# Reordering the opening, the compression products, the memory norm and the sums of squares in a one-core decoder kernel

## Chip, cores and metric

One core of one Trainium2 chip runs the kernel in a single launch. The metric is the device time of that execution in microseconds; the time before is the median of three runs.

## What is computed

x (256 tokens, 1024 features) goes through a first block and two more layers, all in float32. The first block is a mixer, memory attention and a gated convolutional FFN; behind it come a short convolution layer and an mLSTM layer, with 16 meta tokens ahead of the sequence. The parts that the change touches are these, cut from the reference:

```python
h = rms_norm(x, mix_norm_pre[l])
proj = h @ w_in[l]     # q, kc, vc, ks, vs, kw, vw, gates, pool, u, v
...
r = kv.reshape(B, S // 16, 16, G, dk)                    # compress(): of kc and vc
blocks = jnp.concatenate([r[:, :-1], r[:, 1:]], axis=2) + pos
h = jax.nn.gelu(jnp.einsum('bclgd,ldh->bcgh', blocks, w1) + b1)
return jnp.einsum('bcgh,hd->bcgd', h, w2) + b2
...
h = rms_norm(x, mem_norm_pre[l])                         # norm of x1
m = rms_norm(mem, mem_norm_kv[l])
x = x + rms_norm(memory_attention(h, m, w_mq[l], w_mk[l], w_mv[l], w_mo[l]), mem_norm_post[l])
h = rms_norm(x, ffn_norm_pre[l])                         # norm of x2
```

A further rms_norm of this kind stands ahead of the convolution layer (h0) and ahead of the mLSTM (h1).

## The kernel before

**Chunks.** The weights are packed as 288 chunks of 128 x 1024 floats, in the order of use (`_LAYOUT`, L40). Each chunk passes through one of four slots: SyncE loads it (`load`, L497), ScalarE copies it to `w_hi`, rounded (`hi`, L647), VectorE forms the rest `w_lo = raw - w_hi` (`lo`, L1855), and TensorE multiplies. ScalarE's copy of chunk n waits until the product of chunk n-4 is done; the load of chunk n waits for `w_lo` of chunk n-4. The calls `ahead(n)` on ScalarE and VectorE prepare chunk n+3, so the place of each call in the program of an engine sets the order there. Each engine's program is written out by hand and works strictly in order; engines meet through counting semaphores.

**Products.** Activations are split the same way (XH and XL, AH and AL, MH and ML). A chunk of eight 128-row tiles is three products per tile (`three`, L1296 to L1302): high by high, low by high, high by low. `chunk` (L1324) waits for both parts of the weights and runs all eight; `high_first` (L1338) needs `w_lo` only for its last third.

**Opening.** SyncE issues the gains, chunk 0, the halves of x, then chunks 1 to 3. ScalarE splits chunk 0, then the eight tiles of x scaled by the gain (L745); VectorE follows with their rests (L1965). TensorE runs kc with a wait per tile of x, then vc, vs and vw, ks, kw, query 0 (`qa`), the mean squares of the memory, the compression, queries 1 to 3, the gates and the scores.

**Compression.** kc and vc are gathered into `RF` (128 x 1024), rounded to `AH[:, 2048:3072]` (L768), the rest to `AL` (L2003). For each of 16 steps three products with a stationary tile of 64 columns (L1434 to L1436) run against two chunks at once, 256 columns. The result `ch` (64 rows used) is turned by two transposes (L1443, L1444), goes through gelu on ScalarE, and through `cmp_w2` (L1451, L1454).

**Memory.** ScalarE squares the memory (L771). The reciprocal root is spread over the partitions (L1203), copied to `rstd_m` (L792), and VectorE multiplies gain and rstd in eight instructions, three and five (L2043). ScalarE rounds all of it in one instruction during head 0 (L874), GpSimd takes the rest in one instruction (L597). In GpSimd's queue the store of the relative bias (L588) and its four loads (L592), each behind the product of a named chunk, stand ahead of that.

**Heads.** For each of eight heads TensorE runs one weight chunk, the pv products of the head before, qk of the head after, a second chunk, then turns the probabilities (`turn`, L1519 on, transposes at L1526 to L1531). VectorE adds the bias, takes maxima, and after ScalarE's exponentials (L852) scales (L2217). In heads 1 and 2 the chunks are `sgu_u` and `pool`; VectorE takes them out of PSUM (L2171, L2178) at the end of the head, in `fill_late`. Products alternate between two PSUM accumulators, and each waits for the one before the last to be taken out.

**Sums of squares.** A norm needs the mean square of each token. `stat_x` (L1207) runs 32 small f32 matmuls, recorded as 64, four strips of each of eight tiles of squares (`sum_strips`, L1193). It serves x, x1, x2 and h0. `stat_sum` (L1215) takes one tile that GpSimd has added up from seven (`sum_squares`, L542, six adds chained by a semaphore) and the last tile of squares by itself; it serves h1. ScalarE makes the squares in pairs (L688) behind the updated x, which VectorE adds up (L1904, L1949), between rests (L1885).

## Time and profile before

| | us |
|---|---|
| median of three runs | 925.24 (925.12 to 925.93) |
| the profiled execution | 926.31 |
| its span | 924.6 |
| TensorE (PE) busy | 911.6 (99%), 6977 matmul records |
| VectorE (DVE) busy | 657.1 (71%) |
| ScalarE (ACT) busy | 533.1 (58%) |
| GpSimd (POOL) busy | 129.5 (14%) |
| mean DMA | 171 GB/s |

The profile is of one execution. Busy times are of the engine's own instructions; matmuls are pipelined, so that the record of one (0.28 us for 256 columns) is longer than the step from one to the next. L12 is line 12 of the kernel. A row of the timeline gives start, length, engine, line, operation, output and inputs, shapes and count, and in brackets how long the engine sat idle before it and what ended that.

### The profile page before, as it was taken

The numbers are of one execution on the slowest core, as the hardware profiler recorded it, in microseconds if no ns is written. First come the engines' busy times: TensorE is split into PE (matmuls) and PEld (weight loads), VectorE is DVE, ScalarE is ACT, GpSimd is POOL, SyncE is SP. The second block draws the span as 40 slices with busy tenths as digits, with TensorE's granted clock in tenths as the row PEclk, the third lists the DMA queues.
The fourth block names the chain that finished last, engine by engine and source line by source line (L and its number), as shares of the span: only waits on it lengthen the run. The fifth ranks groups of instructions, "written<-read, shape, count | busy, mean of one in ns | idle before, by whom it ended". The sixth has DMA issues, their size and how long they took to land.

```text
span 924.6 us, 19102 instructions
## 1 busy us (share of the span) xinstructions
PE 911.6 (99%) x6977; PEld 856.3 (93%) x6977; DVE 657.1 (71%) x1116; ACT 533.1 (58%) x905; POOL 129.5 (14%) x122
## 2 busy tenths in 40 slices
PE   8999999999999999999999999999999999999997
PEld 7997899998999999889999999999999998888886
DVE  4898877555899997447877777766577566767743
ACT  6767677445776676446444444444454567666643
POOL 2210011000055666000111111101010000000000
PEclk9999999999999999999999999999999999999999
DMA  8752425535356665762655555565465544454561
GB/s 298 260 187 97 155 93 167 174 115 179 124 169 192 200 205 179 229 188 97 196 174 175 176 178 172 175 198 178 142 199 178 170 145 142 159 170 160 182 198 52
DMA packets 45075, 157.91 MB, mean 171 GB/s; under 512 B 6067, under 2 KB 7219, under 8 KB 44764
## 3 DMA queue, kind: packets, MB, share of 16 engines
q1 hardware_dynamic: 44524, 155.56, 51.3%
q0 software_dynamic: 496, 1.59, 0.6%
q8 instruction: 38, 0.62, 0.3%
q14 instruction: 17, 0.14, 0.1%
HBM read 156.06 MB, written 1.06 MB: 170 GB/s over the span
## 4 chain that ended last, share of the span: by engine, by line
PE 93%; DVE 3%; ACT 2%; issue 1%; DMA 1%; SPq 0%; DVEq 0%; ACTq 0%
PE acc L1300 13%; PE acc L1302 13%; PE acc L1301 13%; PE scores L1300 6%; PE scores L1301 5%; PE scores L1302 5%; PE acc L1253 4%; PE acc L1255 4%; PE acc L1254 4%; PE scores L1255 2%; PE scores L1253 2%; PE scores L1254 2%; PE outs L1253 2%; PE outs L1255 2%; PE outs L1254 2%; PE acc L1375 1%
## 5 line engine op out<-in xcount | busy, mean ns | idle before, releaser
L1859 DVE TENSOR_TENSOR w_lo<-raw,w_hi 128x1024 fp32r<-128x1024 f32 x288 | 356.1, 1243 | 98.1 <-ACT w_hi L652 97.6
L652 ACT ACTIVATE w_hi<-raw 128x1024 fp32r<-128x1024 f32 x288 | 302.2, 1056 | 150.4 <-PE acc L1302 64.8
L1300 PE MATMUL acc<-XH,w_hi 128*128 128x256 f32 (+1 forms) x624 | 178.2, 286 | 1.4 <-DVE SQ L2171 1.1
L1301 PE MATMUL acc<-XL,w_hi 128*128 128x256 f32 (+1 forms) x624 | 175.8, 282 | 0.0
L1302 PE MATMUL acc<-XH,w_lo 128*128 128x256 f32 (+1 forms) x624 | 175.8, 282 | 0.0
L1300 PEld LDWEIGHTS acc<-XH,w_hi 128*128 128x128 f32 x624 | 117.4, 188 | 3.9 <-issue 2.1
L1300 PE MATMUL scores<-XH,w_hi 128*128 128x272 f32 (+1 forms) x424 | 120.2, 283 | 0.0
L1301 PE MATMUL scores<-XL,w_hi 128*128 128x272 f32 (+1 forms) x424 | 119.7, 282 | 0.0
L1302 PE MATMUL scores<-XH,w_lo 128*128 128x272 f32 (+1 forms) x424 | 119.7, 282 | 0.0
L1301 PEld LDWEIGHTS acc<-XL,w_hi 128*128 128x128 f32 x624 | 117.5, 188 | 0.1
L1302 PEld LDWEIGHTS acc<-XH,w_lo 128*128 128x128 f32 x624 | 117.4, 188 | 0.0
L1300 PE MATMUL acc<-AH,w_hi 128*128 128x272 f32 (+1 forms) x360 | 103.9, 289 | 0.0
L1302 PE MATMUL acc<-AH,w_lo 128*128 128x272 f32 (+1 forms) x360 | 102.5, 285 | 0.0
L1301 PE MATMUL acc<-AL,w_hi 128*128 128x272 f32 (+1 forms) x360 | 102.5, 285 | 0.0
L1300 PEld LDWEIGHTS scores<-XH,w_hi 128*128 128x128 f32 x424 | 79.7, 188 | 0.2
L1301 PEld LDWEIGHTS scores<-XL,w_hi 128*128 128x128 f32 x424 | 79.8, 188 | 0.0
L1302 PEld LDWEIGHTS scores<-XH,w_lo 128*128 128x128 f32 x424 | 79.8, 188 | 0.0
L1300 PEld LDWEIGHTS acc<-AH,w_hi 128*128 128x128 f32 x360 | 68.0, 189 | 0.1
L1301 PEld LDWEIGHTS acc<-AL,w_hi 128*128 128x128 f32 x360 | 68.0, 189 | 0.0
L1302 PEld LDWEIGHTS acc<-AH,w_lo 128*128 128x128 f32 x360 | 68.0, 189 | 0.0
L629 POOL TENSOR_TENSOR AR<-AR,rstd 128x272 f32<-128x272 f32 x16 | 26.1, 1633 | 216.6 <-DVE AR L2363 216.6
L606 POOL TENSOR_TENSOR AR<-AR 128x256 f32<-128x256 f32 x22 | 32.3, 1470 | 131.6 <-DVE AR L2320 127.0
(533 smaller groups left out, 1797.1 us busy)
## 6 DMA issues: line engine op xcount, KB each, us to landing
raw<-weights SPq DMA_DIRECT2D x288, 512.0 KB, 3.6
cst<-params SPq DMA_DIRECT2D x1, 1080.5 KB, 8.8
XR<-x_t SPq DMA_DIRECT2D x2, 512.0 KB, 6.4
Y<-mem_t SPq DMA_DIRECT2D x1, 1024.0 KB, 7.6
AR<-bias_rows POOLq DMA_DIRECT2D x4, 256.0 KB, 6.4
out<-AR SPq DMA_DIRECT2D x2, 512.0 KB, 2.7
AR<-final_gain POOLq DMA_DIRECT2D x1, 512.0 KB, 7.5
cst<-params SPq DMA_DIRECT2D x1, 114.5 KB, 3.6
```

The source lines that it names most:

```text
L606: nc.gpsimd.tensor_tensor(Ft[:, p % 2, :], Gt[:, p % 2, :], Vt[:, p % 2, :], ALU.mult).then_inc(act_ready, 1)
L629: nc.gpsimd.tensor_tensor(Yc, Yc, rstd[:, :], ALU.mult).then_inc(c_scaled, 1)
L652: nc.scalar.activation(w_hi[:, n % SLOTS, :], raw[:, n % SLOTS, :], ACT.Copy).then_inc(hi_ready, 1)
L1253: nc.tensor.matmul(o, hi, w_hi[:, w, c], start=first, stop=False)
L1254: nc.tensor.matmul(o, hi, w_lo[:, w, c], start=False, stop=False)
L1255: return nc.tensor.matmul(o, lo, w_hi[:, w, c], start=False, stop=last)
L1300: nc.tensor.matmul(o, wh, h, start=start, stop=False)
L1301: nc.tensor.matmul(o, wh, l, start=False, stop=False)
L1302: return nc.tensor.matmul(o, wl, h, start=False, stop=stop)
L1375: nc.tensor.matmul(o, xh(k)[:, b * P:(b + 1) * P], wh, start=(k == 0), stop=False)
L1859: V.tensor_tensor(w_lo[:, s, :], raw[:, s, :], w_hi[:, s, :].bitcast(F32), ALU.subtract).then_inc(lo_ready, 1)
```

## The change

The diff does seven things.

1. SyncE issues the first half of x ahead of chunk 0. ScalarE and VectorE split chunk 0 between the fourth and fifth tile of x. A new `first_chunk` runs the products with `w_hi` of four tiles, then those with `w_lo`, then the other four tiles.
2. Query 1 moves ahead of the compression (`qa` has two chunks, `qb` two); chunk numbers shift, and the bias loads wait for other chunks. VectorE prepares chunk 8 after the keys instead of before.
3. High and low part of the compression input lie side by side in AH, 64 and 64 columns, so each step has one stationary tile of 128 columns and two products (with `w_hi` and `w_lo`). `ch` then has 128 rows; four f32 products with the identity add the halves and turn them.
4. The memory norm goes from VectorE to GpSimd: eight multiplies by the gain ahead of the bias loads, eight by rstd behind them, and the rest in eight pieces.
5. The spread of the memory's rstd moves between the two compression pairs; query 3 moves ahead of `cmp_w2`.
6. `keep_gated` takes the first tile of `sgu_u` and `pool` out before the head's exponentials are awaited, the second right behind the scaling.
7. The sums of squares of x1, x2 and h0 are added up by GpSimd and go through `stat_sum`.

```diff
-_LAYOUT = [("kc", 1), ("vc", 1), ("vsw", 2), ("ks", 1), ("kw", 1), ("qa", 1), ("cmp", 4), ("qb", 3), ...
+_LAYOUT = [("kc", 1), ("vc", 1), ("vsw", 2), ("ks", 1), ("kw", 1), ("qa", 2), ("cmp", 4), ("qb", 2), ...
...
+        RF_hl = AH[:, 2048:4096].rearrange("p (a b c) -> p a b c", a=16, b=2)
...
+            load_x(0)
             load(0)
-            load_x(0)
             load_x(1)
... (GpSimd)
             pool.dma_start(bias_rows, vec[0:HEADS, :]).then_inc(bias_stored, 16)
+            pool.wait_ge(mem_sq, 1)
+            for k in range(KT):
+                nc.gpsimd.tensor_tensor(mem_raw[:, k, :], mem_raw[:, k, :], col("g_mem_kv", k).to_broadcast([P, S]), ALU.mult).then_inc(mem_scaled, 1)
             pool.wait_ge(bias_stored, 16)
-            for j, done in enumerate((CHUNK["qa"], CHUNK["cmp"] + 1, CHUNK["cmp"] + 3, CHUNK["qb"])):
+            for j, done in enumerate((CHUNK["qa"], CHUNK["qa"] + 1, CHUNK["cmp"] + 1, CHUNK["cmp"] + 3)):
...
+            pool.wait_ge(mem_rstd, 1)
+            pool.wait_ge(mem_scaled, KT)
+            for k in range(KT):
+                nc.gpsimd.tensor_tensor(mem_raw[:, k, :], mem_raw[:, k, :], rstd_m[:, 0:S], ALU.mult).then_inc(mem_normed, 1)
             pool.wait_ge(mem_hi, 1)
-            nc.gpsimd.tensor_tensor(ML[:, :, :], mem_raw, MH[:, :, :].bitcast(F32), ALU.subtract).then_inc(mem_lo, 1)
-            pool.wait_ge(mem_lo, 1)
+            for k in range(KT):
+                nc.gpsimd.tensor_tensor(ML[:, k, :], mem_raw[:, k, :], MH[:, k, :].bitcast(F32), ALU.subtract).then_inc(mem_lo, 1)
+            pool.wait_ge(mem_lo, KT)
             nc.gpsimd.memset(pT[:, :, 0:META], 0.0).then_inc(pool_padded, 1)
             sum_squares(lambda m: wait_evacuated(pool, TILE["w_out"] + m), META)
+            for count in (1, 2):
+                sum_squares(lambda m: pool.wait_ge(sq_ready, KT * count + m + 1), META)
...
+            sum_squares(lambda m: pool.wait_ge(sq_ready, KT * 3 + m + 1), 0)
             with pool.Fori(0, E_TILES) as i:
... (ScalarE)
-            hi(0)
             act.wait_ge(gains_loaded, 16)
             for k in range(KT):
+                if k == KT // 2:
+                    hi(0)
...
-            ahead(CHUNK["cmp"] + 1)
+            ahead(CHUNK["cmp"])
             swap(0, "ks")
             swap(1, "kw")
+            ahead(CHUNK["cmp"] + 1)
+            act.wait_ge(rstd_spread, NORM_MEM + 1)
+            nc.scalar.activation(rstd_m[:, 0:S], spread_mem(), ACT.Copy).then_inc(mem_rstd, 1)
             for c in range(2, 4):
                 ahead(CHUNK["cmp"] + c)
-            ahead(query(1)[0])
-            act.wait_ge(rstd_spread, NORM_MEM + 1)
-            nc.scalar.activation(rstd_m[:, 0:S], spread_mem(), ACT.Copy).then_inc(mem_rstd, 1)
... (TensorE)
+            def first_chunk(n, t):
+                s, o, half = n % SLOTS, acc(t)[:, 0:S], KT // 2
+                pe.wait_ge(hi_ready, n + 1)
+                for k in range(half):
+                    x_ready(k)
+                    nc.tensor.matmul(o, w_hi[:, s, k * P:(k + 1) * P], xh(k), start=(k == 0), stop=False)
+                    nc.tensor.matmul(o, w_hi[:, s, k * P:(k + 1) * P], xl(k), start=False, stop=False)
+                pe.wait_ge(lo_ready, n + 1)
+                for k in range(half):
+                    nc.tensor.matmul(o, w_lo[:, s, k * P:(k + 1) * P], xh(k), start=False, stop=False)
+                for k in range(half, KT):
+                    x_ready(k)
+                    last = three(o, n, k, xh(k), xl(k), False, k == KT - 1)
+                last.then_inc(chunk_done, 1)
...
-            chunk(CHUNK["kc"], TILE["kc"], xh, xl, S, ready=x_ready)
+            first_chunk(CHUNK["kc"], TILE["kc"])
...
+            chunk(*query(1), xh, xl, S)
             pe.wait_ge(cmp_in, 1)
...
-                    rows = slice(2048 + 64 * j, 2048 + 64 * (j + 1))
-                    nc.tensor.matmul(o, AH[:, rows], slots(w_hi, n, cols), start=(j == 0), stop=False)
-                    nc.tensor.matmul(o, AL[:, rows], slots(w_hi, n, cols), start=False, stop=False)
-                    last = nc.tensor.matmul(o, AH[:, rows], slots(w_lo, n, cols), start=False, stop=(j == 15))
+                    both = RF_hl[:, j, :, :].rearrange("p a b -> p (a b)")
+                    nc.tensor.matmul(o, both, slots(w_hi, n, cols), start=(j == 0), stop=False)
+                    last = nc.tensor.matmul(o, both, slots(w_lo, n, cols), start=False, stop=(j == 15))
                 last.then_inc(chunk_done, 2)
-            pe.wait_ge(bias_copied, 1)
-            chunk(*query(1), xh, xl, S, between=lambda: spread_rstd(NORM_MEM, S, spread_mem()))
+                if c == 0:
+                    pe.wait_ge(bias_copied, 1)
+                    spread_rstd(NORM_MEM, S, spread_mem())
+            chunk(*query(2), xh, xl, S)
...
-            nc.tensor.transpose(OB[1][:, 0:32], ch[0:32, 0:P], ident[0:32, 0:32])
-            nc.tensor.transpose(OB[0][:, 0:32], ch[32:64, P:S], ident[32:64, 32:64]).then_inc(cmp_hidden, 1)
-            chunk(*query(2), xh, xl, S)
+            for bank, cols, at in ((OB[1], slice(0, P), 0), (OB[0], slice(P, S), 32)):
+                for part in range(2):
+                    last = nc.tensor.matmul(bank[:, 0:32], ch[:, cols], ident[:, 64 * part + at:64 * part + at + 32],
+                                            start=(part == 0), stop=(part == 1))
+            last.then_inc(cmp_hidden, 1)
+            chunk(*query(3), xh, xl, S)
...
-            stat_x(NORM_X1, 1, S)
+            stat_sum(NORM_X1, 2, lambda: pe.wait_ge(sq_ready, 2 * KT), S)
... (the same for NORM_X2 and NORM_H0)
... (VectorE)
-            lo(8)
... (behind keep_keys)
+            lo(8)
             lo(9)
             lo(10)
...
+            def keep_gated(h, j):
+                if h == 1:
+                    n, t = CHUNK["sgu_u"] + j, TILE["sgu_u"] + j
+                    wait_chunk(dve, n)
+                    freed(V.tensor_tensor(uT[:, j, :], acc(t)[:, 0:S], rstd[:, META:T], ALU.mult), t)
+                if h == 2:
+                    n, t = CHUNK["pool"] + j, TILE["pool"] + j
+                    wait_chunk(dve, n)
+                    if j == 0:
+                        dve.wait_ge(mem_lo, KT)
+                    freed(V.tensor_tensor(pT[:, j, META:T], acc(t)[:, 0:S], rstd[:, META:T], ALU.mult), t)
...
                 if h:
                     fill_dve(h - 1)
+                keep_gated(h, 0)
                 dve.wait_ge(exped, h + 1)
...
+                keep_gated(h, 1)
                 if h == 0:
                     compressed_probs()
```

## Rows read from the trace of the kernel before

**Rows 1.** The page: busy time by engine, and the two costliest groups of instructions.

```profile
PE 911.6 (99%) x6977; PEld 856.3 (93%) x6977; DVE 657.1 (71%) x1116; ACT 533.1 (58%) x905; POOL 129.5 (14%) x122
...
L1859 DVE TENSOR_TENSOR w_lo<-raw,w_hi 128x1024 fp32r<-128x1024 f32 x288 | 356.1, 1243 | 98.1 <-ACT w_hi L652 97.6
L652 ACT ACTIVATE w_hi<-raw 128x1024 fp32r<-128x1024 f32 x288 | 302.2, 1056 | 150.4 <-PE acc L1302 64.8
```

**Rows 2.** The waits of PE: for whom, us in total, times, longest.

```profile
PE acc L1300 <- DVE SQ L2171: 1.1, 1, 1.1
PE acc L1300 <- DVE Y L2178: 1.0, 1, 1.0
```

**Rows 3.** The timeline of the opening, ScalarE and PE.

```profile
7.69 3.31 ACT L745 ACTIVATE XH<-XR,cst 128x256 fp32r<-128x256 f32 x8 [1.52 <-DMA XR<-x_t]
...
12.08 0.31 PE L1343 MATMUL acc<-XH,w_hi 128*128 128x256 f32 x1
```

**Rows 4.** The instructions of line 504: ns min/median/max, first and last start.

```profile
L504 SPq DMA_DIRECT2D XR<-x_t x2: 426/466/507, 1.7 to 2.2; - x2
...
DMA to landing us min/median/max: 5.9/6.4/6.8
```

**Rows 5.** The timeline around the compression, PE and ScalarE.

```profile
34.17 0.30 PE L1434 MATMUL acc<-w_hi,AH 128*64 128x256 f32 x1 [0.20 <-DVE AR L2009]
...
39.83 0.28 PE L1436 MATMUL acc<-w_lo,AH 128*64 128x256 f32 x1
...
53.18 1.86 PE L1466 MATMUL turned<-AR 128*128 128x32 f32 x16
...
38.41 1.74 ACT L780 ACTIVATE SQ<-AR 64x256 f32<-64x256 f32 x4
```

**Rows 6.** The instructions of line 606, feed-forward stage: ns min/median/max.

```profile
L606 POOL TENSOR_TENSOR AR<-AR x22: 739/1586/1597, 253.2 to 361.6; 128x256 f32<-128x256 f32 x22
```

**Rows 7.** The timeline of GpSimd, and of VectorE in head 1.

```profile
44.09 0.71 POOL L592 DMA_DIRECT2D AR<-bias_rows  x1 [2.96 <-PE acc L1302]
65.15 4.59 POOL L597 TENSOR_TENSOR ML<-Y,MH 128x2048 fp32r<-128x2048 f32 x1 [20.35 <-ACT MH L874]
...
67.46 3.37 DVE L1859 TENSOR_TENSOR w_lo<-raw,w_hi 128x1024 fp32r<-128x1024 f32 x1 [0.23 <-ACT w_hi L652]
```

**Rows 8.** The page's DMA issues: KB each, median us to landing.

```profile
AR<-bias_rows POOLq DMA_DIRECT2D x4, 256.0 KB, 6.4
```

**Rows 9.** The timeline of head 2, VectorE and PE.

```profile
80.50 1.01 DVE L2217 TENSOR_SCALAR AR<-AR 128x128 f32<-128x128 f32 x4
...
81.62 0.38 PE L1526 MATMUL turned<-ident,AR 128*128 128x128 f32 x2
```

**Rows 10.** The timeline of PE at the sums of squares.

```profile
157.61 1.10 PE L1193 MATMUL outs<-SQ,ones_d 128*32 128x64 f32 x64
158.65 0.38 PE L1300 MATMUL acc<-XH,w_hi 128*128 128x256 f32 x1
...
243.52 1.10 PE L1193 MATMUL outs<-SQ,ones_d 128*32 128x64 f32 x64
...
430.37 1.15 PE L1193 MATMUL outs<-SQ,ones_d 128*32 128x68 f32 x64
...
663.75 0.33 PE L1193 MATMUL outs<-cst,ones_d 128*32 128x68 f32 x8
...
664.12 0.39 PE L1300 MATMUL acc<-XH,w_hi 128*128 128x272 f32 x1
```

**Rows 11.** The timeline of ScalarE at the last squares of x1, x2, h0.

```profile
156.04 0.91 ACT L687 ACTIVATE XH<-XR,cst 128x256 fp32r<-128x256 f32 x2 [0.15 <-DVE XR L1904]
156.86 0.61 ACT L688 ACTIVATE SQ<-XR 128x512 f32<-128x512 f32 x1
...
239.95 0.61 ACT L688 ACTIVATE SQ<-XR 128x512 f32<-128x512 f32 x1
...
426.33 0.64 ACT L688 ACTIVATE SQ<-XR 128x544 f32<-128x544 f32 x1
```

More of the change, by code:

```diff
@@ L1456, in _ @@
             last.then_inc(cmp_out, 1)
-            chunk(*query(3), xh, xl, S)
             chunk(CHUNK["gates"], TILE["gates"], xh, xl, S)
@@ L1684, in _ @@
             side_by_side(3, CHUNK["up"], TILE["up"], up_acc, xh, xl, RAW_X2)
-            stat_x(NORM_X2, 2, S)
+            stat_sum(NORM_X2, 3, lambda: pe.wait_ge(sq_ready, 3 * KT), S)
             ffn_pe(0, 3, lambda: spread_rstd(NORM_X2, S))
@@ L1696, in _ @@
             side_by_side(3, CHUNK["conv_in"], TILE["conv_in"], conv_acc, xha, xla, RAW_H0)
-            stat_x(NORM_H0, 3, T)
+            stat_sum(NORM_H0, 4, lambda: pe.wait_ge(sq_ready, 4 * KT), T)
             conv_pe(0, 3, lambda: spread_rstd(NORM_H0, T))
@@ L2032, in _ @@
             invert_root(NORM_MEM, S)
+            keep_query(1)
             n, t = CHUNK["cmp"], TILE["cmp"]
-            ahead(n + 1)
-            ahead(n + 2)
+            for c in range(3):
+                ahead(n + c)
             wait_chunk(dve, n + 3)
-            freed(V.tensor_copy(ch[0:64, :], acc(t)[0:64, 0:S]), t)
+            freed(V.tensor_copy(ch, acc(t)[:, 0:S]), t)
             ahead(n + 3)
-            def normalise_mem(first, end):
-                for k in range(first, end):
-                    last = V.scalar_tensor_tensor(out=mem_raw[:, k, :], in0=mem_raw[:, k, :], scalar=col("g_mem_kv", k),
-                                                  in1=rstd_m[:, 0:S], op0=ALU.mult, op1=ALU.mult)
-                    if k < KT - 1:
-                        chain.note(last)
-                return last
-            keep_query(1)
-            ahead(query(1)[0])
-            dve.wait_ge(mem_rstd, 1)
-            normalise_mem(0, 3)
             keep_query(2)
             ahead(query(2)[0])
+            keep_query(3)
             dve.wait_ge(cmp_out, 1)
@@ L2632, in _pack_weights @@
     queries = [_tiles(np, q, p) for p in pairs]
-    parts += queries[0:1] + pairs_of("cmp", hidden) + queries[1:4] + [narrow(gt, ar(24))] + pairs_of("sgu_v", lin(v)) + lin(u) + lin(pin)
+    parts += queries[0:2] + pairs_of("cmp", hidden) + queries[2:4] + [narrow(gt, ar(24))] + pairs_of("sgu_v", lin(v)) + lin(u) + lin(pin)
     mv = lin(a["w_mv"][0])
```

36 lines of the change are left out of this document (12 added, 24 removed).

## The prediction

> **What bounds the kernel now.** The profiled execution took 926.31 us, of which 924.6 us is its span; the median of the three runs is 925.24 us. I make the sum against 926.31 and move the result down by 1.07 us to stand with the median. I read the busy shares first: PE is busy 99% of the span [rows 1], so nothing but PE's own products, and the few places where PE waits, can move the end. Then the waits of PE: after the start only two exceed half a microsecond, 1.1 us on a VectorE copy into SQ and 1.0 us on one into Y [rows 2]. Last the timeline of each stage that the diff touches. A difference of 0.2% (1.85 us) is about what a measurement of this kernel can tell from no change.
>
> **Opening.** x now goes out ahead of the first weight tile. Before, ScalarE's copies of x began at 7.69 and took 3.31 us for eight, 0.41 each [rows 3]. The halves of x were issued at 1.7 and 2.2 and landed 5.9 and 6.8 us later, at 7.6 and 9.0 [rows 4]. The three transfers carry the same bytes after, so the last of them, x's second half, still lands near 9.0; only the first half moves, to some point ahead of 7.6. ScalarE's last four copies then end no sooner than 9.0 + 1.65 = 10.65, and VectorE, with w_lo of chunk 0 (1.24) [rows 1] now between its two halves, ends its rests near 11.3. The second chunk, which began at 12.08 [rows 3], begins near 11.75. **Gain 0.3** (0 to 1.0 if the second half lands early too). Cost of the moved weight load: load 4 waits for that w_lo and goes out about 2 us later, hidden behind the three tiles still queued.
>
> **Compression.** 48 products become 32. They run from 34.17 to 39.83, 47 steps, 0.12 us each [rows 5]; with low and high parts side by side in one stationary tile the form is 128 columns, as in all other chunks. Sixteen fewer: 1.93 us. The two small transposes, one pass each, become four f32 products of 128x32 of two passes each; 16 such passes took 1.86 us, 0.116 each [rows 5], so six more cost 0.70. The chunk ahead of it waited 0.20 us for VectorE's key copy [rows 5]; one w_lo moves behind that copy, and the wait goes. Net 1.93 - 0.70 + 0.20 = 1.43.
> What is late next: weight preparation. Chunk 11's slot is free only when the query ahead of the pairs is done. PE then needs it after 16 products and the spread, 1.92 + 1.0 = 2.9 us; ScalarE's copy (1.06) and VectorE's rest (1.24) take 2.3 [rows 1], but the vector queue still holds a query copy and a reciprocal, and GpSimd now runs eight multiplies here. For the next query ScalarE passes four half-tile swaps (1.74 us) [rows 5] before its copy: about 3.2 us against 2.9. I take stalls of **0.8** in all (0 to 1.4). **Gain 0.6** (0 to 1.4).
>
> **Memory normalised by GpSimd.** VectorE loses eight multiplies; GpSimd gets sixteen, and its one subtraction of 4.59 us becomes eight. 4.59 / 8 = 0.57 us per tile; an operation on 256 columns with the port to itself is recorded as 0.74 [rows 6]. The first pass, 5 to 9 us from about 34, stands ahead of the four bias loads in GpSimd's queue; they end near 46.5 instead of 44.8 and land some 6.4 us later [rows 7, 8], before the softmax of head 0 asks near 55. The second pass ends by 55; ScalarE reads the result near 62. So the cover is 7 us, and I cost the lateness at nothing. The contention is another matter: while the single subtraction ran (65.15 to 69.74) a w_lo that started at 67.46 took 3.37 us instead of 1.24 [rows 7, 1]: it stood still until GpSimd was through. Short GpSimd instructions hold it for 0.57 at most, which takes back the small wait ahead of turn(1): **gain 0.25** (0 to 0.3). The last bias load took GpSimd 0.71 us [rows 7], and I cost all four so.
> The Trainium skill (SBUF — State Buffer, section "SBUF: two separate sides") says a load issued by GpSimd grows from about 620 to 3100 ns beside a VectorE copy. By that the four would take 12.4 us and head 0 would wait several us for its bias; the row with 0.71, beside a w_lo on VectorE, decides here.
>
> **Gated tiles sooner.** The 1.1 us and 1.0 us waits [rows 2] are accumulators whose product was long done, freed only at the end of a head. Both go. But after the first, PE reaches turn(2) (81.62) with its probabilities just made, 80.50 to 81.51 [rows 9], by a ScalarE chain (two table loads, four exponentials) that hangs on turn(1), not on this wait. Of 1.1 about **0.45** remains; of the second **1.1** (its next turn has over a microsecond of room). Sum 1.55 (1.0 to 2.2).
>
> **Squares added by GpSimd.** A stage of `stat_x` occupies PE from 157.61 to 158.65, 1.04 us; the two-part form, already used near the end, from 663.75 to 664.12, 0.37 us [rows 10]. Three stages save 0.67 each, if the sum is there. Before x2 and h0 the last squares end at 240.56 and 426.97, PE asks at 243.52 and 430.37 [rows 11, 10]: 3 us of room for at most three adds at 0.74. Gain **1.35** together (-2.5 to 1.35).
> Before x1 there is no room: the last squares end at 157.47, PE asks at 157.61 [rows 11, 10]. Without any contention the last add ends at 158.2, PE goes on at 158.6, and nothing is gained or lost. But there VectorE runs back to back, additions and rests with both inputs in SBUF, and ScalarE's copies for the last pair wait for it (0.15 us) [rows 11]. By the row at 67.46 each add holds VectorE up for 0.57. With turns taken one for one, three adds fall ahead of its last addition: squares near 159.4; the last two adds with one w_lo between them end near 161.0, PE goes on at 161.4. **Loss 2.6** (0 to 3.8).
>
> **Sum.** 0.3 + 0.6 + 0.25 + 1.55 + 1.35 - 2.6 = 1.45. 926.31 - 1.45 = 924.86, or 923.8 beside the median. Own range of this case: 922.3 to 925.3, 0.50, of which 0.10 lies over 0.2% faster.
>
> **Rivals.**
> (1) The port at x1 costs little: the adds slip into VectorE's PSUM reads. For: its scaling instructions read PSUM and, as elsewhere in the trace, were not held. Against: the 3.37 us row. Then x1 costs 0 to 0.5, compression perhaps 1.0: gain 4.3, 921.0. Chance 0.30, all faster.
> (2) Slower: the six chained adds at all three stages. In the feed-forward stage, beside a w_lo, GpSimd's instructions were recorded at 1.59 us in the median rather than 0.74 [rows 6]. At 1.6 per add the chain from the first pair takes 9.6 us: x1 loses 4, x2 (first squares 235.7) asks at 243.52 and gets its sum at 245.3, loses 1.1 net, h0 loses 0.8. That is -5.9 in place of -1.25; with compression at nothing the total is 3.8 slower, 929.0. It decides from an add of about 1.3 us on. Against: VectorE has pauses at x2 and h0 after its last w_lo. Chance 0.10.
> (3) The softmax chain takes all: the freed tiles bring nothing, since ScalarE's chain from turn to turn is the real bound of heads 1 to 3. Gain falls by 1.55 to -0.1: 925.3. Against: PE still has room at turn(3). Chance 0.10, all within 0.2%.
> The Trainium skill (SBUF — State Buffer, section "Who interferes with whom") says whoever issues first keeps the shared pair for its whole instruction; the 3.37 us row agrees. It says nothing of who is next among waiting ones, which is what parts the forecast from rival 1.
>
> **How the numbers follow.** Likeliest case 923.8. Faster: 0.30 + 0.10 = 0.40. Within 0.2%: 0.40 + 0.10, and 0.01 of rival 2's near end: 0.51. Slower 0.09. The range, 920.7 to 926.0, takes in rivals 1 and 3 and leaves out rival 2 and the outer tenth.
>
> **What would show it.** In the profile after: the second chunk begins at 11.5 to 12.0; 32 compression products, with waits of PE on w_lo of 0.3 to 1.4 us around them; no wait on SQ or Y copies in the heads, but one of about 0.5 at turn(2) on VectorE; no w_lo over 2.5 us near 65; a wait of PE on GpSimd's sum before mq of 2 to 3 us (under 0.9: rival 1), none before the feed-forward and convolution (over 1 us: rival 2). I am wrong if waits of PE on w_lo appear beyond 100 us, or if the opening moves by over 1 us.

## The result, and the profile after

| | before | after |
|---|---|---|
| median, us | 925.57 (925.12 to 926.12) | 938.86 (931.3 to 939.6, five runs) |
| ratio | | 1.0127 [1.0105, 1.0149] |
| the profiled execution, us | 926.31 | 931.3 |
| its span, us | 924.6 | 929.4 |

The change makes the kernel slower: by 1.3% in the ratio, by 13.3 us between the medians, where 1.45 us of gain was forecast. The profiled execution of the changed kernel is its fastest; the other four lie at 938.4 to 939.6. So the same kernel was run and profiled again (experiment e0, 936.38 us in that execution), and the two profiles are read side by side. What both show is taken as the price in every execution. What e0 alone shows is taken as what makes most of them slower still, and the mean granted clock of the runs speaks for that: 0.992 to 0.994 of 2.4 GHz in the four slower ones, 0.993 in e0's, 0.997 in that of 931.3.

The page of the execution of 931.3 us. GpSimd has 160.4 us for 129.5 [rows 1], PE 154 fewer records, and yet PE is busy for longer.

```profile
PE 914.3 (98%) x6823; PEld 858.6 (92%) x6823; DVE 661.4 (71%) x1108; ACT 532.8 (57%) x905; POOL 160.4 (17%) x163
L1893 DVE TENSOR_TENSOR w_lo<-raw,w_hi 128x1024 fp32r<-128x1024 f32 x288 | 356.8, 1246 | 95.1 <-ACT w_hi L665 94.6
```

The waits of PE after its start, same execution (for whom; us in total, times, longest). Both waits of [rows 2] are gone, the one of 0.5 at a turn is there (0.6), and a new one of 3.0 on GpSimd's sum for x1.

```profile
PE outs L1207 <- POOL cst L549: 3.0, 1, 3.0
PE acc L1465 <- DVE AR L2063: 0.9, 1, 0.9
PE turned L1560 <- DVE AR L2241: 0.6, 1, 0.6
```

And those of e0, the same kernel at 936.38 us. The first row is new: PE stands 4.7 us ahead of the first compression product, until VectorE has freed query 1's accumulator.

```profile
PE acc L1465 <- DVE AR L2063: 4.7, 1, 4.7
...
PE outs L1207 <- POOL cst L549: 3.0, 1, 3.0
PE acc L1314 <- DVE AR L2063: 0.9, 1, 0.9
```

Where PE stands at six places, read from the timelines, in us. Differences between neighbouring columns say in which stretch the time went.

```text
                              before   after    e0      e17 (best version, below)
sum of x                       17.38    17.34   17.54    17.37
first scores product, head 0   55.33    55.07   62.70    54.58
sums of y                     144.62   143.19  152.24   142.37
sum of x1                     157.61   159.25  168.28   155.37
sum of x2                     243.52   245.58  254.91   241.39
last product                  919.09   923.90  929.07   916.70
```

Three losses can be read off it. (1) In e0, 7.4 us up to head 0, and 1.5 more by the scores of head 1 (62.03 before, 70.94). (2) At x1 about 3 us, in both. (3) From x2's sum to the end: 675.6 us before, 678.3 in the execution of 931.3, but 674.2 in e0. The last is not a wait: the timeline has none there.

**Loss 1, at the memory norm.** GpSimd's and VectorE's timelines in the execution of 931.3: start, length, engine, line. GpSimd's eight gain multiplies take 7.67 us, 0.96 each, and VectorE's three w_lo 4.42. They take turns: a multiply beside a w_lo is recorded at about 1.6 us, one alone at about 0.6, and no w_lo there takes over 1.73.

```profile
33.95 7.67 POOL L593 TENSOR_TENSOR Y<-Y,cst 128x256 f32<-128x256 f32 x8
32.81 4.42 DVE L1893 TENSOR_TENSOR w_lo<-raw,w_hi 128x1024 fp32r<-128x1024 f32 x3
44.55 7.37 POOL L604 TENSOR_TENSOR Y<-Y,rstd_m 128x256 f32<-128x256 f32 x8
```

The same in e0. Now the eight run in 4.60 us, 0.57 each, with nothing between them, and VectorE's two w_lo of 34.44 take 6.86 instead of 2.4: the first of them takes 5.72 and stands still for the whole series. The same happens at 50 us, in the second series.

```profile
34.47 4.60 POOL L593 TENSOR_TENSOR Y<-Y,cst 128x256 f32<-128x256 f32 x8
34.44 6.86 DVE L1893 TENSOR_TENSOR w_lo<-raw,w_hi 128x1024 fp32r<-128x1024 f32 x2 [0.25 <-ACT w_hi L665]
50.02 5.58 POOL L604 TENSOR_TENSOR Y<-Y,rstd_m 128x256 f32<-128x256 f32 x8
50.17 6.52 DVE L1893 TENSOR_TENSOR w_lo<-raw,w_hi 128x1024 fp32r<-128x1024 f32 x1 [0.21 <-ACT w_hi L665]
```

**What a pause costs besides itself.** PE in e0, and by stretch (us; busy of PE, PEld, DVE, ACT, POOL; then PEclk, the granted clock as a share of 2.4 GHz; DMA). Behind the pause the clock is 0.50, 1.2 GHz: products 0.21 us apart instead of 0.12, until about 46.7, some 5 us of work that cost 2.5 more.

```profile
41.77 0.55 PE L1465 MATMUL acc<-w_hi,AH 128*128 128x256 f32 x1 [4.71 <-DVE AR L2063]
...
44.26 0.41 PE L1466 MATMUL acc<-w_lo,AH 128*128 128x256 f32 x1
44.47 0.41 PE L1465 MATMUL acc<-w_hi,AH 128*128 128x256 f32 x1
...
42.00:46.00 4.00, 4.00 (x20) 4.00 (x21) 1.50 (x3) 0.38 (x1) 0.17 (x1) 0.50 0.96 305
46.00:48.00 2.00, 2.00 (x16) 2.00 (x16) 1.22 (x1) 1.64 (x3) 0.55 (x1) 0.82 0.98 371
```

**Loss 2, at x1,** execution of 931.3: PE asked at 156.3 and waited 2.99 us for GpSimd's last add, and here too the clock fell behind the pause. The strip took 0.59 us instead of 0.37, and the next eleven steps 2.44 instead of 1.30: 1.4 more.

```profile
152.79 1.23 DVE L1938 TENSOR_TENSOR XR<-XR,Y 128x512 f32<-128x512 f32 x1
155.63 3.56 POOL L549 TENSOR_TENSOR cst<-cst,SQ 128x256 f32<-128x256 f32 x3 [2.16 <-ACT SQ L701]
156.01 1.75 DVE L1893 TENSOR_TENSOR w_lo<-raw,w_hi 128x1024 fp32r<-128x1024 f32 x1
159.25 0.44 PE L1207 MATMUL outs<-cst,ones_d 128*32 128x64 f32 x8 [2.99 <-POOL cst L549]
...
160.00:162.00 2.00, 2.00 (x10) 2.00 (x11) 1.32 (x3) 1.72 (x3) 0.00 (x0) 0.50 0.40 141
```

**Loss 3, the spacing of products.** The same stretch of the feed-forward loop, before and after, PE 100% busy at a clock of 1.00 in both: 796 products against 767 in 90 us.

```profile
260.00:350.00 90.00, 90.00 (x796) 90.00 (x795) 84.34 (x136) 63.12 (x103) 54.42 (x34) 1.00 0.61 198
```

```profile
260.00:350.00 90.00, 90.00 (x767) 90.00 (x766) 80.30 (x131) 60.52 (x98) 50.13 (x33) 1.00 0.56 187
```

The starts of successive products lie 0.1133 us apart before and 0.1178 after, all through the loop (means over 946 and 950 steps, from 250 us on). 960 products by 0.0045 us is 4.3 us; less the 1.35 that the two shorter sums save, this makes 2.9, beside the 2.75 by which the stretch from x2's sum to the end is longer in the execution of 931.3. e0 has the shorter spacing: it lost more in front and less here. Both levels occur in either kernel in earlier stages; what differs is which one the loop is run at.

### The profile page after: what moved, and what is told of

It reads as the page before. It is cut to its first block, busy times and chain, and to the rows that moved or that the text cites. A ratio compares the mean times of both kernels' runs of the same rounds, so it can differ in the third digit from the quotient of the medians.

```text
span 929.4 us, 18833 instructions
## 1 busy us (share of the span) xinstructions
PE 914.3 (98%) x6823; PEld 858.6 (92%) x6823; DVE 661.4 (71%) x1108; ACT 532.8 (57%) x905; POOL 160.4 (17%) x163
## 3 DMA queue, kind: packets, MB, share of 16 engines
q0 software_dynamic: 496, 1.59, 0.6%
## 4 chain that ended last, share of the span: by engine, by line
PE 91%; DVE 4%; ACT 2%; issue 1%; DMA 1%; POOL 0%; SPq 0%; DVEq 0%; ACTq 0%; POOLq 0%
PE acc L1314 13%; PE acc L1316 13%; PE acc L1315 13%; PE scores L1314 6%; PE scores L1316 6%; PE scores L1315 6%; PE acc L1269 4%; PE acc L1267 4%; PE acc L1268 4%; PE scores L1269 2%; PE scores L1268 2%; PE scores L1267 2%; PE outs L1269 2%; PE outs L1268 2%; PE outs L1267 2%; DVE w_lo L1893 1%
## 5 line engine op out<-in xcount | busy, mean ns | idle before, releaser
L642 POOL TENSOR_TENSOR AR<-AR,rstd 128x272 f32<-128x272 f32 x16 | 26.2, 1634 | 156.3 <-DVE AR L2388 156.3
L1269 PE MATMUL acc<-w_hi,AL 128*128 128x512 f32 x128 | 49.9, 390 | 0.0
```

Source lines behind the costliest of these rows:

```text
L642: nc.gpsimd.tensor_tensor(Yc, Yc, rstd[:, :], ALU.mult).then_inc(c_scaled, 1)
L1269: return nc.tensor.matmul(o, lo, w_hi[:, w, c], start=False, stop=last)
```

## The experiments

The first theory, on record ahead of e0 to e3, was built on the execution of 931.3 alone: x1's sum comes late, the pause brings the clock down, and perhaps the loop's spacing hangs on it. It had nothing at the memory norm. The theory that the later runs test has three sources. A, a back-to-back series of GpSimd holds VectorE's w_lo up, as if the whole series were one instruction; B, x1's chained adds come too late; and both pauses bring the clock down; C, the spacing of the loop's products turns. In the expectations "theory A" is the theory of that run, and what it says stands beside it. Rivals are named with each run. Diffs are against the changed kernel unless said otherwise.

**e0, the changed kernel again; e1, x1's sum back on TensorE; e2, all three sums back; e3, the kernel before with one more warming product.**

```diff
# e1 (e2 does the same at x2 and h0)
-            stat_sum(NORM_X1, 2, lambda: pe.wait_ge(sq_ready, 2 * KT), S)
+            stat_x(NORM_X1, 1, S)
# e3, against the kernel before, ahead of the feed-forward loop
-            keep_warm(1, PTB)
+            keep_warm(2, PTB)
```

> The changed kernel as it is, for the spread of its times and a second trace. Theory A (three costs in a row: PE waits 3.0 us for GpSimd's sum before mq; this pause drops the granted clock to half for 3.4 us; the feed-forward loop then runs at 0.1178 us per 256-column product instead of 0.1133, 4.3 us): the trace shows the wait of 3 us again, and the times that lie near 939 are those in which the clock stays at half for longer than 3.4 us. Rival B (something far from the norm, for example weight preparation late in the long loops): waits of PE on w_lo beyond 250 us that the first trace does not have.

> The changed kernel with the sum of squares before mq on PE again (stat_x), the other two still with GpSimd. Theory A: the 3 us wait goes, the clock stays at full speed, and about 2.65 + 1.7 us come back; if the pitch of the loop hangs on the pause too, another 4.3 us: 921 to 927, and all executions close together. Rival B: still above 930, or executions still 8 us apart.

> The changed kernel with all three sums of squares on PE again. Against e1 it should be 1.3 us slower if the sums before the feed-forward stage and before the convolution save 0.67 us each as worked out, and no different if they don't. If the pitch of the feed-forward loop flips with it, 4.3 us more or less on top, to be read from the trace.

> The kernel before with one more warming product (128 columns, two passes) ahead of the feed-forward loop, nothing else. If the pitch of the loop's products has two levels and what stands ahead of the loop picks one (theory C), its 960 products may run at 0.1178 us instead of 0.1133: 4.3 us slower, 929.5. If the level hangs on something else (the pause, the clock), this kernel costs only its own 0.15 us: 925.5.

Measured, beside 926.29 for the kernel before: e0 937.15 (ratio 1.0119 [1.0091, 1.0147]), e1 935.49 (1.0101 [1.0084, 1.0118]), e2 930.34 (924.83 to 933.08, 1.0039 [1.0019, 1.006]), e3 930.62 (1.0045 [1.0028, 1.0062]). e3 settles what the spacing is worth, and that one more small product ahead of the loop can turn it: its four runs lie at 930.19 to 932.18, the lowest three about 4 us above the kernel before, and its loop shows the spacing of after.

```profile
260.00:350.00 90.00, 90.00 (x767) 90.00 (x766) 79.63 (x131) 60.05 (x97) 49.54 (x33) 1.00 0.57 187
```

e0 has the wait of 3 us at x1 again and its low clock, as expected, but not the longer spacing, and no wait on w_lo beyond 250 us (rival B falls). What that theory had nothing about is the wait of 4.7.

e1 and e2 removed the wait at x1, and both traces brought the large wait at the compression (4.4 and 4.7 us), which the first profile hadn't shown. e1 missed its 921 to 927 by 8 us: its rival (still above 930) holds, and the x1 sum is not the main loss. e2 was expected 1.3 us above e1 and lies 5.1 below it. Its trace has the loop at 0.1133, that of e1 at 0.1178, so putting the sums of x2 and h0 back turned the spacing as well.

```profile
260.00:350.00 90.00, 90.00 (x797) 90.00 (x795) 84.67 (x138) 64.02 (x105) 53.74 (x35) 1.00 0.58 189
```

Two of e2's ten runs, at 924.83 and 925.01, had a mean clock of 0.999 and 1.000 where the other eight had 0.994 to 0.996. They have no profile, but it looks as if the series at the memory norm cost nothing in them.

**e6, GpSimd's gain multiplies spaced; e14, both series spaced; e15, both spaced and x1's sum on TensorE.**

```diff
# e6; e14 and e15 do the same in the second series, with mem_normed
             for k in range(KT):
+                if k:
+                    pool.wait_ge(mem_scaled, k)
                 nc.gpsimd.tensor_tensor(mem_raw[:, k, :], ... ALU.mult).then_inc(mem_scaled, 1)
```

> The changed kernel with one wait more: each of GpSimd's eight gain multiplies waits for the one before it, so the series is no longer queued back to back. Theory A (while a back-to-back series of GpSimd runs, VectorE's w_lo beside it stands still: it took 4.6 us in the executions near 937 and not in the one at 931.3): each gap lets VectorE in, no w_lo there takes over 2 us, TensorE's wait for the accumulator of query 1 (before the first compression product) is 0 to 1.2 us instead of 4.5, the clock holds at 2.4 GHz from 40 to 48 us, and the time is 930 to 933, in every execution. Theory B (who gets the port first is chance, spacing does nothing): the wait stays at 4.4 us and the time at 937 to 939.

> The changed kernel with both of GpSimd's memory series spaced: every multiply waits for the one before it. Theory A (back-to-back series lock VectorE out): no w_lo of over 2.5 us between 32 and 56 us, no wait of TensorE over 1.2 us before 60, the first scores product at 55 to 56.6, and a median of 930 to 933, no run over 936 but by a turned product spacing. Rival (spacing changes only the odds of one execution): 937 to 939 in half of the runs, and a w_lo of over 5 us in the trace.

> As e14, with the sum of x1's squares back on TensorE. It differs from e10_best (926.7, lowest 922.1) only in that GpSimd normalises the memory, spaced. Theory A (spaced, GpSimd's share costs what VectorE's turns beside it cost, 0.4 to 1.7 us a piece): 925 to 929. Rival (GpSimd's memory work costs the 4 us and the clock behind it whether spaced or not): 931 to 935, as e1 with the series unspaced (935.5).

Measured: e6 932.3 (928.41 to 939.61; 1.0049 [1.0034, 1.0063]), e14 932.14 (929.81 to 933.77; 1.0068 [1.0056, 1.008]), e15 928.77 (924.21 to 931.3; 1.0017 [1.0001, 1.0034]). A wait of each multiply for the one before, which adds work, makes the kernel 6.7 us faster: 938.86 to 932.14, and 935.49 (e1) to 928.77 (e15). The intervals of the ratios don't touch; against e0's median of 937.15 the first difference is 5.0. e14 and e15 lie in the ranges that theory A gave; e6's runs leave its 930 to 933 on both sides. e14's waits of PE and its w_lo beside the series:

```profile
PE outs L1211 <- POOL cst L549: 3.0, 1, 3.0
PE acc L1469 <- DVE AR L2067: 1.2, 1, 1.2
...
34.23 3.32 DVE L1897 TENSOR_TENSOR w_lo<-raw,w_hi 128x1024 fp32r<-128x1024 f32 x2 [0.25 <-ACT w_hi L669]
```

No w_lo stands still (the two take 1.77 and 1.63), and the 4.7 is 1.2. The same can be counted over all traces: beside eleven series of multiplies queued back to back (two each in after, e0, e1, e2 and e8, one in e6) seven times a w_lo took 3.4 to 6.8 us; beside five spaced ones (e6, e14, e15) the longest took 1.8. e6, which spaces the first series alone, has both in one trace. This is its second:

```profile
46.17 6.55 POOL L606 TENSOR_TENSOR Y<-Y,rstd_m 128x256 f32<-128x256 f32 x8
48.73 3.40 DVE L1895 TENSOR_TENSOR w_lo<-raw,w_hi 128x1024 fp32r<-128x1024 f32 x1 [2.37 <-ACT w_hi L667]
```

Being queued back to back is not enough by itself, though. The eight subtractions near 65 us, of the same shape and with no wait between them either, run beside a w_lo in fourteen traces, and it took 1.57 to 1.59 us in every one. This is that of the execution of 931.3:

```profile
64.89 6.60 POOL L607 TENSOR_TENSOR ML<-Y,MH 128x256 fp32r<-128x256 f32 x8 [12.96 <-ACT MH L888]
67.21 1.59 DVE L1893 TENSOR_TENSOR w_lo<-raw,w_hi 128x1024 fp32r<-128x1024 f32 x1 [0.23 <-ACT w_hi L665]
```

Behind e6's long w_lo PE waited 1.1 us at 54.3, and the clock fell. e6's one run at 939.61 was its profiled one. It has no long wait at the first compression product, but besides this one another kind of loss: from 455 to 677 us its products of 272 columns stood 0.1267 us apart, where every other trace has 0.1233 (1423 products against 1462 in 180 us). That is 1750 steps by 0.0033, 5.8 us.

```profile
460.00:640.00 180.00, 180.00 (x1423) 180.00 (x1422) 131.32 (x203) 74.79 (x92) 24.36 (x15) 1.00 0.53 175
```

**e8, the kernel before with only the memory norm moved to GpSimd; e7, the changed kernel with it back on VectorE; e9, e7 with x1's sum on TensorE too.**

```diff
# e7, e9: VectorE again, as in the kernel before
+            dve.wait_ge(mem_rstd, 1)
+            normalise_mem(0, 3)
             keep_query(2)
...
             ahead(query(3)[0])
+            normalise_mem(3, KT).then_inc(mem_normed, 1)
```

> The kernel before with the memory normalised by GpSimd as the change does it (gain multiplies ahead of the bias loads, reciprocal-root multiplies behind them), and nothing else. The prediction costed this at 0.25 and a gain of 0. Theory A (the series holds the port): a w_lo between 33 and 46 us takes 4 to 8 us, TensorE waits 3 to 4.5 us for w_lo or for an accumulator with a drop of the clock behind it, and the time is 928 to 933. Rival (the old order gives VectorE the slack that the new one takes): no wait over 1 us there, 925 to 926.

> The changed kernel with the memory normalised by VectorE, at the two places of the kernel before (three steps behind the compression's copy, five behind the compressed keys and values); everything else of the change stays. Theory A (GpSimd's memory work is what costs): the wait ahead of the first compression product is gone or under 1 us, the only long wait of TensorE left is the 3.0 us for the x1 sum with its 3.4 us at half clock, and the time is 929 to 932. Theory B (the reordered compression itself leaves VectorE late, GpSimd or not): the wait of over 3 us stays, and the time is 935 or more.

> The changed kernel with two parts undone: the memory normalised by VectorE, and the sum of x1's squares left to TensorE. What stays: opening, compression in two products, gated tiles, sums of x2 and h0 by GpSimd. If the two parts undone are the whole loss, the rest gives what was forecast for it: 0.3 + 0.6 + 1.55 + 1.35 = 3.8 at most, so 922 to 923.5 where the 256-column products of the feed-forward loop go 0.1133 us apart, and 926.5 to 928 where they go 0.1178 apart. If something else of the change also costs, 929 or more at the faster spacing.

e8: 926.43 (925.5 to 929.46; 1.001 [1.0001, 1.0019]). The mechanism shows in its purest form, with VectorE's instruction started 0.14 us before GpSimd's series and outlasting it:

```profile
44.50 5.57 POOL L602 TENSOR_TENSOR Y<-Y,rstd_m 128x256 f32<-128x256 f32 x8
44.36 6.79 DVE L1867 TENSOR_TENSOR w_lo<-raw,w_hi 128x1024 fp32r<-128x1024 f32 x1
...
PE acc L1308 <- DVE AR L2036: 1.4, 1, 1.4
```

but the old order of the compression leaves PE more work to do meanwhile. 0.6 us is lost between the medians, 0.9 by the ratio: the median lies below theory A's 928 to 933 and above the rival's 925 to 926, and the profiled run, at 928.05, has its wait of 1.4 with the clock at 1.00. e7 gave 933.64 (1.0072 [1.0057, 1.0087]) and e9 928.87 (1.0031 [1.0021, 1.0042]), 1.6 and 0.9 us above the upper ends of what was expected. The wait of 4.7 is gone, but the place that I gave the last five multiplies made the gates' evacuation late:

```profile
PE outs L1498 <- ACT AR L815: 1.5, 1, 1.5
...
48.00:60.00 12.00, 10.47 (x84) 9.53 (x83) 10.61 (x25) 5.71 (x10) 0.00 (x0) 0.86 0.57 203
```

A fault of my experiment, and a useful one: behind the short products here a pause of 1.5 us brings the clock to 0.50, for 3.4 us in e9's trace (0.86 over these 12) and for 6.8 in e7's. The place is fragile: in e3, whose code here is that of the kernel before, a pause of 0.47 was followed by the same in the profiled execution (932.18, the slowest of its four), so were e15's 0.6 and e6's 1.1, and e14's 0.6 was not. It is also where e0 lost its 1.5 us ahead of head 1.

**e4, x1's sum alone; e5, gated tiles alone; e12, compression alone; e13, opening alone** (each against the kernel before; e12 is the compression part of the diff with VectorE's five late multiplies right behind `keep_query(2)`, where it had been idle for 1.8 us; GpSimd's rest of the memory stays in eight pieces, as in the change).

> The kernel before with one edit: the squares of x1 added by GpSimd, TensorE's 64 one-column products replaced by one strip behind GpSimd's last add. The prediction's term: TensorE goes on 2.6 us late, 0.7 of it given back by the shorter sum. Theory A (the last three adds are held by VectorE's wide instructions, and the pause of 3 us brings TensorE's clock to 1.2 GHz for 3.4 us behind it, 1.7 us more): wait on GpSimd's add 2.5 to 3.1 us, clock row 160:164 under 0.8, time 928.5 to 930. Rival (the clock loss seen in the changed kernel comes from elsewhere in it): clock stays 1.00, time 927 to 928.

> The kernel before with one edit: the four gated tiles evacuated one at a time ahead of the softmax work. The prediction's term: waits of 1.1 and 1.0 at 73.8 and 83.5 gone, a new one of about 0.5 at the turn of head 2, together 1.55 gained: 923.9 to 924.3. In the changed kernel the landmarks moved by 1.34 and 0.34 at these two places, 1.7 in sum. Rival (ScalarE's softmax takes the gain, as the prediction's third rival has it): 925.3 or more. If the one-column or 256-column spacing flips behind it, 4.3 more on either.

> The kernel before with the compression part alone: two products of 128 rows a step, query 1 drawn ahead of it, hidden values as accumulated products; the memory normalised by VectorE at its idle times, opening, gated tiles and all sums as before. The prediction's term: 1.43 saved of products less 0.8 of stalls on w_lo, so 0.6 gained, 0 to 1.4: TensorE reaches the first scores product 0.6 earlier, 54.7 for 55.33, and the time is 925.1. Theory A (the traces of e10_best, where it came at 54.5 with the opening in it): 54.5 to 54.9. Rival (the w_lo stalls take all): 55.3 or later. If the 256-column level turns, 4.3 us more in the time, so that the landmark decides.

> The kernel before with the opening part alone: x ahead of the first weights on SyncE's queue, the first chunk's w_lo products of the first half behind its w_hi products. The prediction's term: 0.3 gained. In the changed kernel TensorE reached the sum of x at 17.34 for 17.38, so theory A says nothing is gained: landmark within 0.15 of 17.38, time within 0.2% of before. Rival (the prediction's): 17.1, time 925.3 to 925.5.

| | median, us | ratio | in the stretch behind it, by trace | forecast |
|---|---|---|---|---|
| e4 x1's sum | 930.94 (929.51 to 931.91) | 1.006 [1.0045, 1.0074] | 3.7 lost (sums of y to sum of x2: 98.9 before, 102.6) | 2.6 lost |
| e5 gated tiles | 924.90 | 0.9992 [0.9983, 1.0001] | 0.9 gained (144.62 to 143.70) | 1.55 gained |
| e12 compression | 924.81 | 0.999 [0.9981, 0.9998] | 1.05 gained (55.33 to 54.28) | 0.6 gained |
| e13 opening | 925.83 | 1.0001 [0.9993, 1.001] | nothing (17.38 to 17.39) | 0.3 gained |

Each of these stretches is read from one trace, and the same code doesn't come to the same place to within 0.3 us: e4, unchanged up to there, reaches head 0 at 54.87, e3 at 55.51, the kernel before at 55.33. The medians say the same as the traces for e5 (0.9 gained), e12 (1.1) and e13 (0.05).

e4 has the wait and the clock of loss 2 in a kernel that is otherwise the old one, so both belong to x1's sum (theory A there; the clock's rival falls):

```profile
PE outs L1194 <- POOL cst L547: 3.0, 1, 3.0
...
160.00:164.00 4.00, 3.58 (x32) 3.41 (x32) 3.32 (x4) 1.75 (x3) 0.36 (x1) 0.57 0.61 218
```

Its profiled run is the fastest of the four, 3.2 us above before's; the median is 5.2 above the one of its own round and 0.9 above the expected range, and what makes up the rest has no trace. In e5 both old waits go, and two new ones come at the turns of heads 1 and 2, since the evacuation now stands ahead of the scaling that PE waits for:

```profile
PE turned L1526 <- DVE AR L2219: 1.1, 2, 0.6
```

**e10, the best set; e11, the same with two warming products; e16, e10 without the opening; e17, compression and gated tiles alone** (with the norm on VectorE and the eight pieces as in e12).

```diff
# e10: e9, with the five late multiplies moved
             keep_query(2)
+            normalise_mem(3, KT).then_inc(mem_normed, 1)
             ahead(query(2)[0])
... (and gone from behind ahead(query(3)[0]))
```

> The last kernel (changed, memory normalised by VectorE, x1's sum on TensorE) with the five late memory steps moved from ahead of the gates' evacuation to VectorE's idle 1.8 us behind the evacuation of query 2. Theory A (those five steps made TensorE wait 1.5 us for the gates, and the clock at 0.86 from 48 to 60 us took 1.4 to 1.7 more): wait gone, clock 1.00, 3 us less: 925 to 926 where the feed-forward loop goes at 0.1178 us a product, 921 to 923 where it goes at 0.1133. Rival (the clock falls there for the accumulated small products, wait or not): clock stays at 0.86, 1.5 less: 926.5 to 928.5.

> The kernel of e10_best with two warming products ahead of the feed-forward loop instead of one. In the kernel before this alone turned the spacing of the loop's 256-column products from 0.1133 to 0.1178 us. Theory C (the level at the loop's entry is turned by what stands ahead of it): it turns here too, so that this kernel and e10_best lie 4.3 us apart, one at 921 to 923, the other at 925 to 927. Rival (in the changed kernel the level varies from execution to execution and the extra product does not decide it): both kernels show both groups of times, with medians within 1.5 us.

> The kernel of e10_best with the opening as before: compression in two products, gated tiles, sums of x2 and h0 by GpSimd, memory on VectorE, x1's sum on TensorE. The sum of what the traces gave for the parts: 1.05 + 0.92 + 1.32 = 3.3, so 922.5 where the feed-forward loop goes at 0.1133. Theory D (the opening sets the level's chance): all runs at 922 to 923. Rival (it is the sums or the gated tiles): runs between 922 and 929 as in e10_best, median 924 to 927.

> The kernel before with compression in two products and the gated tiles one at a time, and nothing else. 1.05 + 0.92 = 2.0 from the two parts alone, less if the second evacuation wait moves: 923.6 to 924.2 at 0.1133. Rival (two parts moved together already turn the level): 928 in some or all runs.

| | median, us | ratio | runs |
|---|---|---|---|
| e10 | 926.73 | 1.0008 [0.9997, 1.0019] | 922.06, 924.79, ten from 926.17 to 928.89 |
| e11 | 924.12 | 0.999 [0.9975, 1.0005] | six from 922.35 to 923.53, six from 924.71 to 928.58 |
| e16 | 926.57 | 0.9998 [0.9988, 1.0008] | 922.59, 922.93, ten from 926.17 to 927.24 |
| e17 | 923.89 | 0.9973 [0.9963, 0.9983] | nine from 923.22 to 923.99 |

In e10 the wait of 1.5 us is gone and with it the low clock, as its theory A had it, and the median is 2.1 us below e9's; at 926.73 it is 0.7 above the range for the longer spacing:

```profile
48.00:60.00 12.00, 12.00 (x110) 11.44 (x109) 11.18 (x31) 7.22 (x16) 0.00 (x0) 1.00 0.53 189
260.00:350.00 90.00, 90.00 (x766) 90.00 (x765) 80.03 (x131) 61.06 (x99) 49.23 (x34) 1.00 0.55 191
```

e10 and e16 have two groups of runs about 4 us apart, and e11's spread over the same stretch; the profile of e10 is one of 927.06 with the loop at 0.1178, that of e11 one of 922.72 at 0.1133. The warming product, decisive in e3, does not decide here: both groups occur with one and with two, as e11's rival has it, though with medians 2.6 us apart rather than 1.5. Whether it shifts the odds (one or two of e10's twelve runs in the fast group, six or seven of e11's) twelve runs don't show. e15 has the two groups too, three runs at 924.2 to 924.5 and nine from 927.03 up. The opening doesn't set them (theory D falls: two of twelve without it too). e17 lacks the sums of x2 and h0, and all its runs lie within 0.8 us, its trace at the shorter spacing. All traces taken together: with x2's sum added up by GpSimd the loop runs at 0.1178 in nine of eleven (not in e0 and e11), without it at 0.1133 in eight of nine (not in e3). So it is with the change of that sum, and of the products just ahead of the loop, that the second level comes in. Why is not shown. In the traces of e1, e9, e15 and e16 the loop's first 95 steps are of 0.1136, and the spacing turns to 0.1178 at one longer step of 0.21 to 0.22, where its second pass begins; in that of e10 it is 0.1178 from the start; in e0 the step there is 0.20 and nothing turns. **e17 beats both kernels**, 0.27% under the kernel before, inside the 923.6 to 924.2 that was expected from its two parts.

## Why the prediction was wrong

- **Memory normalised by GpSimd: the step that failed most.** It read a single instruction of 4.59 us rightly as one that holds a w_lo for its length, and concluded "Short GpSimd instructions hold it for 0.57 at most". Eight short ones, queued with nothing between, held a w_lo for 4.5 to 5.6 us, as if they were one. Spacing them gives back 6.7 us (5.0 against e0's median), and again 6.7 with x1's sum on TensorE; in e0's trace it is 4.7 of wait and 2.5 of clock. For the rest in eight pieces, near 65 us, the sentence held: the w_lo there takes 1.59 for the 3.37 of before. So the step that failed is that the bound of one short instruction was taken to hold for any series of them. The gain of 0.25 did not come: the small wait ahead of turn(1) is 0.20 after and 0.16 before. The passage on lateness ("I cost the lateness at nothing") looked at who waits for GpSimd, and not at who is held by it.
- **A pause has a second price.** No term had the clock in it. In the kernel before the granted clock was 1.00 up to the last 3 us, and after its start it had no pause of over 1.1 us; those of 4.7, 3.0 and 1.5 us in the later kernels were each followed by products at 1.2 GHz.
- **x1's sum.** "PE goes on at 161.4", a wait near 3 us: measured 3.0, with a w_lo beside the last adds, as in the working. PE came to this place 1.4 us sooner than before, and went on to its next product at 159.84, where the working with that lead has 160.0. The term was 2.6 and came to 3.5 in the execution of 931.3, 3.7 in e4's trace and 5.2 in e4's median: the clock was missing, 1.4 of it.
- **Squares of x2 and h0.** No wait on either, so rival 2 (adds of 1.6 us at all three stages) is not what happened, though it is the one whose time, 929.0, lay nearest. From x2's sum to the last product e11 has 674.25 us against 675.57: 1.32 gained for 1.35. But with this edit the loop runs at 0.1178 in nine traces of eleven, at 4.3 us, so its net is a loss; e10 and e16 have ten of twelve runs in the slower group. This is a term that the prediction did not have: it took the products of the loop for as long as before.
- **Gated tiles.** Forecast 1.55, in which the second wait was credited with 1.1, though its row has 1.0; 0.9 alone, 1.2 within the change (55.07 to 143.19 against 55.33 to 144.62). The wait expected at turn 2 came (0.62); a second, at the turn before (0.49 for 0.16 in e5; 0.20 in the changed kernel), was overlooked. Rival 3, that all of it is lost, falls.
- **Compression.** 0.6 was forecast with stalls of 0.8; alone it gave 1.05, with one wait of 0.45 on w_lo. The stalls were sized too high, the mechanism is right. In the changed kernel itself the stall is another one: 0.85 on query 1's accumulator, and none on w_lo.
- **Opening.** Forecast 0.3. VectorE's last rest ended at 11.56, not 11.3: it had stood idle for 0.44 us until chunk 0's w_hi was there, and its w_lo then lay ahead of the last four rests, up to 9.9. The second chunk began at 12.07 for 12.08. Nothing gained.
- **The sum.** Against the kernel before, e0 loses 7.37 up to head 0 (with the compression's gain inside) and 1.54 up to head 1, gains 1.29 up to the sums of y, loses 3.77 up to x2's sum, and gains 1.41 behind it: 10.0, its 936.38 against 926.31. The execution of 931.3 has -0.26, 0.01, -1.18, +3.49 and +2.75: 4.8. No profile fell on one of the runs at 938.4 to 939.6; e0 with the turned spacing would come to 940.7, and without its loss ahead of head 1 to 939.1, among them (an estimate from the differences above); that this is what they are was not shown.

The bound "I am wrong if waits of PE on w_lo appear beyond 100 us" was not met: there are none. The sign given for x1, a wait of 2 to 3 us, came. The other two losses lie in places that the list of signs did not name: a wait at 41 us, on an accumulator, and no wait at all in the loop.

## What to carry to other kernels

Many short instructions of GpSimd queued back to back can hold up an instruction of VectorE as one long one would. It happened in seven of eleven series of multiplies here and in none of fourteen of subtractions, so one clean trace is no proof of safety. If they must run beside VectorE's critical work, let each wait for the one before. Price a pause of TensorE at its length plus the slow products behind it, and look for whoever is held, not only for whoever is late. When a change removes small products ahead of a long loop, compare the step from product to product inside the loop before believing any other explanation, and run the kernel often enough to see whether its times fall into groups.

## What the runs showed of the hardware

- **GpSimd and VectorE side by side.** The same eight multiplies beside the same w_lo ran in two ways in the same kernel: alternating (0.96 us each in the mean, 7.67 in all, no w_lo over 1.73) and closed (0.57 each, 4.60 in all, a w_lo 4.5 us longer; the second series 0.70 each, 5.58, a w_lo 5.3 to 5.6 longer). What decides between them is open; the eight subtractions near 65 us alternated in all fourteen traces that have them. The order of the starts alone does not: by its record the w_lo that was held had started ahead of the series in e0 (34.44 and 34.47) and in e8 (44.36 and 44.50), and in e8's first series, where it started 0.04 us ahead of GpSimd, it was not held.
- **The clock.** After pauses of 1.5 to 4.7 us the granted clock was 0.50 (1.2 GHz) for some 3 to 7 us of work and then 1.00 again (3.4 us at 0.50 in after, e4, e9 and e14, 6.8 at e0's longest pause and in e7). After waits of 1.0 to 1.4 us with full-size products around them (before, e14, e8) it stayed 1.00; among the small products ahead of head 0 it fell behind waits of 0.5 and 0.6 in two traces (e3, e15) and behind one of 0.6 not (e14).
- **Two spacings at one clock.** 256-column products ran at 0.1133 or 0.1178 us a step, 272-column ones at 0.1233 or, in one of twenty traces (e6), 0.1267, with the granted clock at 1.00 and PE without a wait. Beyond the first pass of the feed-forward loop (96 products) the level was not seen to change; it turned at small products between chunks, and in four traces at one step of 0.21 to 0.22 us where the second pass begins. Why the kernels with x2's sum on GpSimd show both levels was not settled, nor whether the kernel before ever shows the longer one: of its 114 runs beside the experiments the highest is 929.88, 4 us above the median, and has no profile.
